# Token rows of the fixed experts by one-hot products, those of later turns gathered through a slot table

## The reference

```python
g_idx = argmax(u @ w_group + b_group)
e_in = (u @ w_router + b_router) of the group g_idx          # 4 logits
top_v, top_i = top_k(e_in, 2)
w = softmax(top_v) * p_group
ids = g_idx * 4 + top_i
h = silu(u @ w_gate[e]) * (u @ w_up[e]) * gate[e]            # gate[e] is 0 where e isn't picked
y = sum over e of h @ w_down[e]
```

## The kernel before

| position | 0 | 1 | 2 | 3 | 4 | 5 | 6 | 7 | 8 | 9 | 10 | 11 | 12 | 13 | 14 | 15 |
|---|---|---|---|---|---|---|---|---|---|---|---|---|---|---|---|---|
| capacity | 96 | 96 | 96 | 96 | 64 | 32 | 96 | 64 | 96 | 64 | 96 | 64 | 96 | 64 | 32 | 32 |
| tokens, layer 0 | 44 | 44 | 71 | 96 | 47 | 16 | 84 | 43 | 74 | 41 | 72 | 38 | 62 | 22 | 7 | 7 |
| tokens, layer 1 | 39 | 58 | 74 | 85 | 46 | 30 | 69 | 42 | 67 | 39 | 49 | 38 | 49 | 37 | 30 | 16 |

## Time and profile before

### The profile page before, as it was taken

The page is one execution under the profiler, slowest core; times in us unless marked ns, Lnnn a source line. Parts: engine busy times, 40 slices in busy tenths (PEclk is TensorE's granted clock), DMA queues, the critical chain, the costliest instruction groups (busy, mean ns, idle before and its releaser), DMA issues.

```text
span 1223.0 us, 23538 instructions
## 1 busy us (share of the span) xinstructions
PE 1114.9 (91%) x10201; PEld 622.1 (51%) x10201; DVE 389.9 (32%) x1023; ACT 233.9 (19%) x501; POOL 140.8 (12%) x163
## 2 busy tenths in 40 slices
PE   5899999899989959988889999999998995998986
PEld 3443445555575535545455555545666553555543
DVE  3201331574251300111233633587624230101104
ACT  2002201321231111101053232321012111111112
POOL 1043100022120000000010000042232000000001
PEclk9999999999989989999999999999998998999998
DMA  9998755359559998999996202002395999899994
GB/s 385 398 304 288 312 206 209 145 174 406 200 233 336 405 386 331 371 395 417 416 324 209 73 16 69 1 1 69 153 360 218 367 407 383 324 374 398 406 419 176
DMA packets 73018, 338.24 MB, mean 277 GB/s; under 512 B 6740, under 2 KB 16243, under 8 KB 58128
## 3 DMA queue, kind: packets, MB, share of 16 engines
q1 hardware_dynamic: 60760, 299.14, 63.2%
q0 software_dynamic: 10864, 36.42, 8.6%
q10 hardware_dynamic: 1288, 1.14, 0.3%
HBM read 314.24 MB, written 22.44 MB: 275 GB/s over the span
## 4 chain that ended last, share of the span: by engine, by line
PE 68%; DMA 18%; DVE 7%; issue 2%; ACT 2%; SPq 1%; POOL 1%; ACTq 0%; DVEq 0%; POOLq 0%
PE ps L2359 16%; DMA ring<-in_moe_w_up 12%; PE ps L1987 11%; PE ps L2562 10%; PE ps L2065 8%; PE ps L2383 7%; PE ps L2622 3%; DMA ring<-in_rec_w_in 3%; PE ps L2008 2%; PE ps L2292 2%; PE ps L2592 1%; PE ps L2342 1%; PE ps L2369 1%; PE ps L1980 1%; ACT work L1183 1%
## 5 line engine op out<-in xcount | busy, mean ns | idle before, releaser
L2359 PE MATMUL ps<-ring,work 128*32 128x256 f32 x4736 | 295.8, 394 | 53.4 <-DMA ring<-in_moe_w_up 49.3
L2359 PEld LDWEIGHTS ps<-ring,work 128*32 128x32 f32 x4736 | 150.4, 113 | 152.4 <-issue 66.3
L2562 PE MATMUL ps<-uT,ring 128*128 128x386 f32 x384 | 128.8, 488 | 0.9 <-issue 0.9
L2383 PE MATMUL ps<-ring,work 128*32 128x256 f32 x1728 | 103.0, 380 | 2.1 <-DVE work L1814 2.1
L2562 PEld LDWEIGHTS ps<-uT,ring 128*128 128x128 f32 x384 | 71.7, 190 | 49.6 <-issue 2.4
L1814 DVE COPY work<-ps 128x128 f32<-128x128 f32 x74 | 21.5, 291 | 235.4 <-PE ps L2369 234.3
L2065 PE MATMUL ps<-uT,ring 128*128 128x384 f32 x256 | 89.2, 505 | 3.0 <-DMA ring<-in_rec_w_in 1.9
L1195 ACT ACTIVATE work<-ps 128x128 f32<-128x128 f32 x74 | 20.5, 277 | 337.0 <-PE ps L2359 337.0
L1987 PE MATMUL ps<-ring,uT 128*128 128x512 f32 x192 | 84.1, 595 | 0.0
L2383 PEld LDWEIGHTS ps<-ring,work 128*32 128x32 f32 x1728 | 55.8, 110 | 39.8 <-DVE work L1814 3.0
L1810 DVE TENSOR_TENSOR work<-ps,work 128x128 f32<-128x128 f32 x74 | 21.6, 292 | 155.6 <-ACT work L1195 155.6
(11 more groups left out here) (371 smaller groups left out, 1194.9 us busy)
## 6 DMA issues: line engine op xcount, KB each, us to landing
ring<-in_moe_w_gate SPq DMA_DIRECT2D x32, 2048.0 KB, 12.8
ring<-in_moe_w_up SPq DMA_DIRECT2D x32, 2048.0 KB, 18.0
ring<-in_ada_w SPq DMA_DIRECT2D x24, 2048.0 KB, 11.3
ring<-in_moe_w_down SPq DMA_DIRECT2D x22, 2048.0 KB, 24.1
uT<-in_moe_w_down SPq DMA_DIRECT2D x10, 1536.0 KB, 16.4
ring<-in_rec_w_in SPq DMA_DIRECT2D x6, 2048.0 KB, 23.5
ring<-in_hy_w_in SPq DMA_DIRECT2D x6, 2048.0 KB, 13.4
y_rows<-work SPq DMA_DIRECT2D x64, 96.0 KB, 12.7
```

Source lines behind the costliest of these rows:

```text
L2359: ins = pe.matmul(bank(key)[32 * q:32 * q + 32, 0:2 * P].rearrange("p (a n) -> p a n", a=2), xg[:, u, k, 32 * i:32 * i + 32], ring[:, 3 * ...
L2383: ins = pe.matmul(bank(key)[32 * q:32 * q + 32, 0:256], hT[:, (FIRST[p] + i) % 2, 32 * k:32 * k + 32], w[:, q * 256:(q + 1) * 256], start= ...
L2562: ins = pe.matmul(bank(key)[:, 0:T + 2], w[:, k, (m % 4) * P:(m % 4 + 1) * P], uH[:, k, :], start=(k == 0), stop=(k == DC - 1))
```

## The change

Positions 1 and 2 get their rows as position 0 does: DVE writes the 0/1 table of expert 1 and later of expert 2 into the same `oh0`, and `rows_t` makes 24 products for each instead of 8 transposes. Tokens are stored once, in token order, by three plain writes, and no longer scattered. Instead, POOL scatters one number of 4 bytes per pick (token number minus 384, `less`) into a slot table in DRAM, reads the part of the table that belongs to positions 3 to 15 back in three transfers, adds 384, and fetches the rows of a position by an indirect DMA with these numbers. Empty slots hold 0, so their number is 384, which is out of bounds, and they are skipped. The zero fill of `x_rows` shrinks to one of the two slot tables. SyncE's wait at position 0 is gone. Two of POOL's clears share one (not shown), and in the overflow path tokens are reloaded directly (not shown).

```diff
@@ -139,7 +139,7 @@
         tc_ = sb("tab_common", [P, 3 * P + NT + 4 + NE])
         ident, strict, iota = tc_[:, 0:P], tc_[:, P:2 * P], tc_[:, 2 * P:3 * P]
         o = 3 * P
-        tokid, w4, obase = tc_[:, o:o + NT], tc_[:, o + NT:o + NT + 4], tc_[:, o + NT + 4:o + NT + 4 + NE]
+        less, w4, obase = tc_[:, o:o + NT], tc_[:, o + NT:o + NT + 4], tc_[:, o + NT + 4:o + NT + 4 + NE]
         ones = sb("ones", [P, P])
         eps = sb("eps", [P, 1])
         vecT = sb("vecT", [P, V_ALL])
@@ -159,6 +159,7 @@
 
         late = sb("late", [P, 6 * NT])
         x_dram = nc.dram_tensor("x_rows", [XROWS + 1, D], F32).ap()
+        slot_dram = [nc.dram_tensor(f"slot_tokens_{l}", [XROWS, 1], F32).ap() for l in range(2)]
         y_dram = nc.dram_tensor("y_rows", [XROWS, D], F32).ap()
         shift_dram = nc.dram_tensor("shift_rows", [2, 2, D], F32).ap()
         gate_dram = nc.dram_tensor("gate_rows", [2, D], F32).ap()
...
@@ -517,6 +518,8 @@
         here, wl, slot = (a.get(2 * NT).rearrange("p (q j) -> p q j", q=2) for _ in range(3))
         rts = a.get(2 * P, parts=96)
         oh0 = a.get(NT * CAP).rearrange("p (j s) -> p j s", j=NT)
+        slot_less = a.get(RANKS)
+        slot_token = a.get(RANKS).bitcast(U32)
         a.at = 3840
         diag = a.get(2 * D).rearrange("p (v m n) -> p v m n", v=2, m=DC)
         a.at = 9216
...
@@ -690,9 +693,6 @@
                     ahead_by = 3 if p < AHEAD else 2
                     after = expert_at(p + ahead_by)
                     full(sp, (l, p, "GU", TILES[p] - 1))
-                    if p == 0:
-                        sp.wait_ge(S("rows1_loaded"), 16 * (l * (NE // 2) + 1))
-                        sp.wait_ge(S("rows0_loaded"), 16 * (l * (NE // 2 - 1) + 1))
                     load_part(0, e, u)
                     load_part(1, e, u)
                     if p != AHEAD:
...
@@ -832,9 +832,8 @@
                 pool.dma_start(b20[:, l, NG:], A["moe_b_router"][l].partition_broadcast(P)).then_inc(S("router_loaded"), 16)
             clear(A_sb, "A_cleared")
             pool.wait_ge(S("zeros_cleared"), 1)
-            for a0, p_, n in ((0, P, ROWS // P), (ROWS // P * P, ROWS % P, 1)):
-                pool.dma_start(x_dram[a0:a0 + p_ * n, :].rearrange("(p a) (h n) -> p (a h) n", p=p_, n=512),
-                               bc(zeros[0:p_].unsqueeze(1), [p_, 2 * n, 512])).then_inc(S("x_rows_cleared"), 16)
+            for l in range(2):
+                pool.dma_start(slot_dram[l][0:ROWS, 0].rearrange("(p n) -> p n", p=32), zeros[0:32, 0:ROWS // 32]).then_inc(S("slots_cleared"), 16)
 
 
             pool.wait_ge(S("gla_exp"), 2)
@@ -901,21 +900,33 @@
 
             def moe(l):
 
-                pool.wait_ge(S("rows_known"), l + 1)
-                if l == 0:
-                    pool.wait_ge(S("x_rows_cleared"), 32)
                 for n, j in enumerate(BY_ROWS):
                     pool.wait_ge(S("u_rows"), NT * l + n + 1)
+                    pool.dma_start(x_dram[j * P:(j + 1) * P, :], utok[:, j, :]).then_inc(S("row_tables"), 16)
+                pool.wait_ge(S("rows_known"), l + 1)
+                pool.wait_ge(S("slots_cleared"), 32)
+                for j in range(NT):
                     for q in range(2):
-                        pool.indirect_dma_start(x_dram, bass.IndirectOffsetOnAxis(ap=ridx[:, j, q:q + 1], axis=0),
-                                                utok[:, j, :], None).then_inc(S("x_rows_stored"), 16)
-                pool.wait_ge(S("x_rows_stored"), 16 * 2 * NT * (l + 1))
-
-                for p in range(1, NE):
-                    u, n = p % 2, CAPS[p]
-                    if p >= 2:
+                        pool.indirect_dma_start(slot_dram[l], bass.IndirectOffsetOnAxis(ap=ridx[:, j, q:q + 1], axis=0),
+                                                less[:, j:j + 1], None).then_inc(S("row_tables"), 16)
+                pool.wait_ge(S("row_tables"), 16 * (12 * l + 9))
+                sizes = list(zip((0,) + SMALLER, SMALLER + (RANKS,)))
+                for a0, a1 in sizes:
+                    n, at = rank_cap(a0), FIXED * CAP + sum(rank_cap(b) for b in range(a0))
+                    pool.dma_start(slot_less[0:n, a0:a1], slot_dram[l][at:at + n * (a1 - a0), 0].rearrange("(r s) -> s r", s=n), allow_slow_non_contiguous=True).then_inc(S("row_tables"), 16)
+                pool.wait_ge(S("row_tables"), 16 * (12 * l + 12))
+                for a0, a1 in sizes:
+                    n = rank_cap(a0)
+                    ins = pool.tensor_scalar(slot_token[0:n, a0:a1], slot_less[0:n, a0:a1], float(T), None, ALU.add)
+                ins.then_inc(S("slot_token"), 1)
+                pool.wait_ge(S("slot_token"), l + 1)
+
+                for p in range(FIXED, NE):
+                    u, n, rank_ = p % 2, CAPS[p], RANK_AT[p]
+                    if p >= FIXED + 2:
                         full(pool, (l, p - 2, "X", 1))
-                    pool.dma_start(ug[0:n, u, :], x_dram[BASES[p]:BASES[p] + n, :]).then_inc(S(f"rows{u}_loaded"), 16)
+                    pool.indirect_dma_start(ug[0:n, u, :], None, x_dram[0:T, :],
+                                            bass.IndirectOffsetOnAxis(ap=slot_token[0:n, rank_:rank_ + 1], axis=0), bounds_check=T - 1, oob_is_err=False).then_inc(S(f"rows{u}_loaded"), 16)
 
                 pool.wait_ge(S("picks_known"), l + 1)
                 for u in range(2):
...
@@ -1715,9 +1729,15 @@
                 free(v.tensor_copy(pos4, bank(("pos", l))[:, 0:4 * NE].rearrange("p (j e) -> p j e", j=4)), ("pos", l))
                 evacuated(v, ("pos", l))
                 v.wait_ge(S("mask"), l + 1)
-                for j in range(NT):
-                    ins = v.tensor_scalar(oh0[:, j, :], iota[:, 0:CAP], pl[:, j, 0:1], mask[:, j, 0:1], ALU.is_equal, ALU.mult)
-                ins.then_inc(S("first_slots"), 1)
+
+                def fixed_slots(p):
+                    if p:
+                        full(v, (l, p - 1, "X", 1))
+                    for j in range(NT):
+                        ins = v.tensor_scalar(oh0[:, j, :], iota[:, 0:CAP], pl[:, j, p:p + 1], mask[:, j, p:p + 1], ALU.is_equal, ALU.mult)
+                    ins.then_inc(S("first_slots"), 1)
+
+                fixed_slots(0)
                 for j in BY_ROWS[1:]:
                     add_shift_rows(j)
                 cnt = pos4[:, NT, :]
...
@@ -1750,6 +1770,7 @@
                     if q == 0:
                         chain(ins)
                 ins.then_inc(S("rows_known"), 1)
+                fixed_slots(1)
                 v.wait_ge(S("exp_out"), l + 1)
                 chain(v.tensor_reduce(esum, R5[1][:, :, 0:4], AX.X, ALU.add))
                 e5 = R5[1][:, :, 4:5]
...
@@ -1819,6 +1840,7 @@
                 hidden(0, 2)
                 hidden_t(0, 1)
                 rows_in(1)
+                fixed_slots(2)
                 for p in range(1, NE - 1):
                     for i in range(TILES[p]):
                         if i:
...
@@ -2334,8 +2356,18 @@
                 def rows_t(p, h):
                     u, n_ = p % 2, CAPS[p]
                     key = (l, p, "X", h)
+                    if p < FIXED:
+                        pe.wait_ge(S("first_slots"), FIXED * l + p + 1)
+                        opened(pe, key)
+                        for n, j in enumerate(BY_ROWS):
+                            for q in range(4):
+                                k = 4 * h + q
+                                ins = pe.matmul(bank(key)[:, q * CAP:(q + 1) * CAP], utok[:, j, k * P:(k + 1) * P], oh0[:, j, :],
+                                                start=(n == 0 and q == 0), stop=(n == NT - 1 and q == 3))
+                        done(ins, key)
+                        return
                     if h == 0:
-                        pe.wait_ge(S(f"rows{u}_loaded"), 16 * (l * (NE // 2 - 1 + u) + p // 2 + u))
+                        pe.wait_ge(S(f"rows{u}_loaded"), 16 * (l * (NE // 2 - 2 + u) + (p - 2) // 2 + u))
                     opened(pe, key)
                     for n in range(4):
                         k = 4 * h + n
@@ -2384,7 +2416,7 @@
                                             w[:, q * 256:(q + 1) * 256], start=(k == 0), stop=(k == 3))
                     done(ins, key)
 
-                pe.wait_ge(S("first_slots"), l + 1)
+                pe.wait_ge(S("first_slots"), FIXED * l + 1)
                 for h in range(2):
                     opened(pe, (l, 0, "X", h))
```

More of the change, by code:

```diff
@@ L75, in tables @@
         np.eye(P), (i[:, None] < i[None, :]), np.tile(i, (P, 1)),
-        i[:, None] + P * np.arange(NT)[None, :], np.tile([4, 3, 2, 1], (P, 1)),
+        i[:, None] + P * np.arange(NT)[None, :] - T, np.tile([4, 3, 2, 1], (P, 1)),
         np.tile(ROWS - CAP + P * np.arange(NE), (P, 1))], axis=1).astype(np.float32)
@@ L793, in _ @@
             clear(zeros[:], "zeros_cleared")
-            clear(gkw, "gkw_cleared")
+            clear(gkw, "rec_small_cleared")
             clear(g36, "g36_cleared")
-            clear(mcol, "mcol_cleared")
```

(14 more changed lines are left out.)

## The result

The changed kernel takes 1244.51 us (median of 12 runs, 1238.96 to 1253.11), the kernel before beside it 1234.55: ratio 1.0092, 95% interval 1.0066 to 1.0119. One of the 12 runs of before took 3899.99 us; without it the median is 1234.11. A second timing (e12) gave 1.0076 [1.0044, 1.0107]. The change makes the kernel slower by about 10 us; the two intervals allow 8 to 15 and 5 to 13 us. The profiled execution took 1242.73 us (span 1240.9).

A forecast was written before the change was run, and what follows sets the result against it. PE was taken to pace experts up to position 4, the weight stream from position 6. Layers of +4.3 and +4.5 gave +8.8 us: 1233.7 for the profiled execution, 1243.8 for a median run, 0.7% slower, range 1232 to 1254.

The forecast's parts named there:

- Products: PE, experts 1 and 2: 5.4 us each replacing transposes, adding 8.7 us in layer 0 and 8.4 in layer 1.
- paid at position 6: SyncE's weight issues from position 3 to 6 come later with PE; position 6's gate load 8 to 9 us later.
- What the stream gives back: Weight stream: backlog 2.1 (1.6) us, then skipped rows 0.5 and 1.8 us in layer 0, 0.6 and 1.7 in layer 1.
- the backlog of 2.1 (1.6) us is used up first: Older transfers queued before position 5's gate load absorb 2.1 us of PE's delay in layer 0, 1.6 in layer 1.
- The sum: Both layers: +4.3 us in layer 0 and +4.5 in layer 1, together +8.8 us.
- Slot table: POOL's scatter, read and gather chain: position 3's rows arrive at 388.7 to 399.5, wanted at 403.5, so it costs nothing.
- SyncE's wait worth 0: SyncE at position 0: removing the wait frees 5 us for SyncE, which bring nothing by themselves.
- Swallowed and faster: Rival, weight stream: PE's spare waits absorb the delay and skipped rows cut time to 1230.4 or 1216 us; chance 0.15.
- Nothing given back: Rival, weight stream: skipped rows cost as much as fetched, backlog forms again, 17.1 us pass in full: 1252.1; chance 0.14.
- It cancels: Rival, PE after its long wait: shorter waits keep the clock up, saving 7.2 us: 1236.6, no visible change; chance 0.13.
- Late rows: Rival, slot table chain: scatters and reads take 24.0 us each, position 3's rows 20 us late: 1264; chance 0.06.
- The base: Starting time: profiled execution of 1224.85 us, 10.1 us below the runs' median of 1234.98, so the forecast was shifted up.

The follow-up runs named there:

- e12: The change itself, unmodified, timed again beside the kernel before, on the chip of e11: 1244.82 us, ratio 1.0076.
- e6: The kernel before, unchanged, profiled a second time: 1238.09 us.
- e7: The kernel before, unchanged, profiled a third time: 1236.26 us.
- e2: The kernel before without SyncE's two waits for row loads at position 0: ratio to before 1.0014.
- e1: The kernel before with products for experts 1 and 2 and no SyncE wait; old scatters and plain loads from position 3 stay: 1255.19 us, ratio 1.0176.
- e8: The change, unmodified, profiled again: 1242.05 us.
- e4: The change with slot table rows of 512 bytes instead of 4: 1245.44 us, ratio to before 1.0106.
- e3: The change with empty slots fetching a row of zeros instead of being skipped: 1252.6 us, ratio to before 1.0139.
- e5: The change with expert 2's rows by slot table and gather, products for experts 0 and 1 only: 1239.55 us, ratio to before 1.0057.
- e10: The change with expert 2's product computed twice, same result: 1242.43 us beside 1224.09 of before on that chip, ratio 1.0162.
- e11: e9 with SyncE's wait of the kernel before put back: 1241.59 us, ratio to before 1.0053.
- e9: The change without products for experts 1 and 2, whose rows go by bounded scatters and plain loads: 1243.59 us beside 1224.09 of before, ratio 1.0163.

## Why the prediction was right, and where it was not

The forecast was 1243.8 us, 0.7% slower; measured were 1244.5 us and 0.92% [0.66, 1.19]. To compare like with like, I cut each layer of every profile at two gate loads: from the start of expert 0's products to position 3's (the stretch that holds the products), and from position 6's to the last one (the stretch paced by the weight stream). Between them, from position 3's to position 6's, all kernels take 48 us in layer 0 and 49 to 50 in layer 1. Each value is from one profile: the same kernel and layer differ by up to 3.7 us in the last column, and expert 0's products, common to all, take 7.2 to 8.8 us.

| us, layer 0 / layer 1 | to position 3 | position 6 to last |
|---|---|---|
| before, first profile | 42.6 / 42.7 | 157.5 / 155.5 |
| before, e6 | 46.2 / 47.8 | 159.4 / 156.7 |
| before, e7 | 45.5 / 45.7 | 155.7 / 154.8 |
| e2, no SyncE wait | 47.8 / 47.7 | 157.6 / 154.9 |
| e1, products only | 57.4 / 57.2 | 158.5 / 157.7 |
| after | 55.6 / 54.8 | 152.4 / 149.8 |
| after, e8 | 54.8 / 57.2 | 151.5 / 150.6 |
| after, e12 | 55.4 / 57.1 | 152.2 / 148.8 |
| e4, wide slots | 55.7 / 54.8 | 153.6 / 149.4 |
| e3, empties read | 54.9 / 55.1 | 156.4 / 157.6 |
| e5, one product | 50.1 / 50.4 | 154.0 / 153.4 |
| e10, two and one double | 55.6 / 57.0 | 154.2 / 148.7 |
| e11, none, skipping | 53.1 / 53.8 | 154.1 / 153.3 |
| e9, the same, no wait | 58.7 / 56.7 | 155.4 / 152.6 |

*Products: right, a little short.* Each took 5.60 to 5.84 us for 5.42. With the transposes off, PE gets 9.5 us more per layer (5.60 + 5.84 - 0.88 - 1.10), forecast 8.7 and 8.4, which also took off the short waits. In the table, after less before (e6, e7, e2) is 55.8 - 46.8 = 9.0 us. The clock held, and each instruction took 0.117 us.

*That it is paid at position 6: right.* The stretch between is unchanged, so all of it reaches the gate load of position 6. From the start of expert 0's products to that load the change takes 103.3 us in layer 0 (mean of three profiles), the old PE program 94.5 (e6, e7, e2): 8.8 later, in the forecast's 8 to 9.

*What the stream gives back: the size right within 2 us, the split wrong.* The forecast was 4.4 us in layer 0 and 3.9 in layer 1, some half of it backlog. Measured: before has 156.5 (mean of e6, e7 and e2, both layers), after 150.9, so 5.6.

The step that failed is "the backlog of 2.1 (1.6) us is used up first". It was read off the first profile of before, where position 5's gate load lands after 10.0 us. In e6, e7 and e2 it lands after 8.8, 9.4 and 7.8, and in the three profiles of the change, 9 us of PE later, still after 9.3, 9.4 and 9.1: PE's delay did not empty that queue (layer 1: 8.6, 8.3, 8.7 before, 8.6, 9.3, 8.3 after). Position 6's up load needs 21.9 us in layer 0 and 20.0 in layer 1 before (means of e6, e7, e2), 21.2 and 19.5 after. The 0.7 and 0.5 us gained there are what the forecast had for skipped rows (0.5 and 0.6), and no backlog. e1, which has the products and reads every row, needs 21.7 and 20.5, and its last stretch has 158.1, nothing back at all (its profile, 1262.22 us, is the slowest of its five runs, but their median says the same: 22 us for 19 of products).

So what comes back goes with skipping. How much that is, for the 2.3 us a layer of the forecast, is not settled. e3 has the products too and reads empties, 157.0 for the 150.9 of the change: 6.1 us a layer by these profiles. The timed runs of e3 say 3, with 2.6 to either side. Without products the stretch of e9 and e11 is 153.9, 2.6 below before. Whether skipping is worth more behind products stays open.

*The sum.* 9.0 - 5.6 = 3.4 us per layer, 7 in all; forecast 8.8. The timed medians differ by 10.0 (1244.51 - 1234.55) and the repeat by 10.3, so some 3 us are not in the two expert stages of these profiles, or in the spread of single executions; the profiles don't tell which. That the forecast of 1243.8 lies 0.7 us from 1244.5 is in part luck: by the stages the delay was forecast 0.4 us a layer too short and the return 1.5 us a layer too short, and the 3 us that the stages don't explain go the other way.

*Slot table: right, with more cover than given.* Position 3's rows were in at 382.7, where the forecast had 388.7 to 399.5. From the first read's issue to the additions it took 3.9 us, where 8.2 were taken. The rule on transfers under 512 bytes (the Trainium skill, DMA: Bandwidth & Descriptors, Specifications) agrees with the 4.30 against 1.56 us of e4, and neither reaches the end: 1.0106 against 1.0092.

*SyncE's wait worth 0: right for this change, for a reason that I hadn't seen.* It guards the row loads of positions 1 and 2 from position 2's weights. In the change there are no such loads. In e2 they go out at 364.75 and the weights, held by the trickle, at 371.67. In e9, where nothing held them, PE stood 14.4 and 13.4 us. The prediction called the wait 5 us of lateness that brings nothing; it is a guard that costs nothing. The lateness itself was smaller in the two later profiles: in e6 the load goes out at 367.89 with the last tile of expert 0 done at 367.8, in e7 at 370.54 with 368.2. The page DMA: Bandwidth & Descriptors of the Trainium skill says, under Queues, rings and completion order, that each DMA engine takes turns between the queues it has work for, packet by packet. The trace of e9 agrees, and shows why turns didn't help: from 376 to 380 us SyncE's queue moved 70 packets with 1.15 MB and POOL's 65 with 0.25 MB, so a turn of the weights is some 16 KB and one of the rows 4 KB. From 370 to 372 it was 53 packets with 0.80 MB against 50 with 0.02 MB, the 4-byte slot numbers that had been issued ahead of the rows. The row load landed at 381.0, with 4.05 MB of the weights moved. From 366 to 370 POOL's queue moved only 3 packets against 65; no row shows what kept it then.

*The rivals.* Swallowed and faster: refuted, the kernel is slower and PE's wait for position 6's up load only fell from 13.3 to 12.1. Nothing given back: that is e1, at 1.0176. It cancels: the first half tile after the wait still takes 3.61 us, so no clock came back. Late rows: no wait of PE names them.

*The base.* The working was made against a profile without the trickle and shifted up by 10.1 us to the median of the runs, without knowing what the 10 us were. That held because the trickle costs both kernels about the same, 4 to 6 us a layer; that it would was not foreseen, which is luck too. Read straight, the first profiles of the two differ by 17.9 us, of which about 8.5 are trickle (11.2 and 11.6 us for expert 0's first 128 gate/up instructions after, 7.1 twice before).

## What to carry to other kernels

Time added to the pacing engine ahead of a prefetch stream is paid when the stream is next the bound; here 9 us went in per layer, and in e1, which cuts no bytes of the stream, none came back. Compare stage by stage with a second profile of the old kernel before reading a difference of 1%: one execution lay 10 us off. And before deleting a wait that costs nothing, look at which small transfer it keeps ahead of a large one.

## What the runs showed of the hardware

*PE's instructions in drops.* In both expert stages of eleven profiles, PE got mostly 4 or 5 instructions per 1.44 us, from 4.6 to 6.9 us after the start of POOL's first indirect scatter on. With 6 scatters it ended 2.0 to 2.3 us after the start of the last one (e6: 358.18 and 360.31), in all 20 stages. With 12, in e11, it ended 1.8 and 1.9 us after it: at 369.67 in layer 0, with the last scatter at 367.88, and at 951.0 in layer 1, with the last at 949.16. In some stages the clock then costs something too: in layer 1 of e6 the granted clock was 0.50 (1.2 GHz) from 941.1 to 943.0, behind a trickle from 937.9 on, and the last 60 of the 128 instructions took 5.26 us, against 3.66 in layer 0, where it was 1.00. On the chip of e9 and e10 the trickle was absent in all four stages, with 12 scatters as with 6, and before ran at 1224 us there and at 1234 elsewhere. The load of the DMA engines doesn't decide it: from 357 to 362 us their busy share was 0.92 in the first profile of before, without a trickle, 0.87 in e6 and 0.02 in the change, both with it. In e11 they moved only 54 GB/s from 362 to 372:

```profile
362.00:372.00 10.00, 7.03 (x57) 2.42 (x58) 0.71 (x3) 0.55 (x2) 5.65 (x7) 0.87 0.40 54
```

That the scatters hold up the fetching of instructions is what these times suggest; no run took the scatters away, so it is argued and not shown, and why one chip is free of it is open.

*Skipped rows.* An out-of-range index in a gather saved its transfer: 5.65 MB in POOL's queue from 360 to 640 us, against 6.82 in e3, where these indices point to a row. The 1.17 MB are the 287 empty slots of positions 3 to 15 in layer 0, at 4 KB each.
